# Second input projection by rows of the contraction, values by token, and one table slot for every side step

## The reference, cut to what matters

```python
h = rmsnorm_2(x, norm_mix_g[l])
proj = jnp.einsum('bsd,de->bse', h, w_in[l])          # 256 x 2048 by 2048 x 7568
c_q, c_kv, k_rope, dq, dk, dv, iq, ik, iw, gates = jnp.split(proj, splits, axis=-1)
# widths: 512, 256, 64, 1024, 256, 256, 1024, 64, 16, 4096
o_a = mla_branch(c_q, c_kv, k_rope, positions, ...)   # rmsnorm of c_q, c_kv; w_uq, w_uk, w_uv; rope; 8 heads
o_b = dsa_branch(dq, dk, dv, iq, ik, iw, positions)   # rope; index scores of 16 heads, top 64 keys of each query; 8 heads
merged = gate[:, :, 0, :] * (o_a @ w_branch_a[l]) + gate[:, :, 1, :] * (o_b @ w_branch_b[l])
x = x + merged @ w_out[l]                             # then the expert layer (peer_ffn) and a last rmsnorm
```

## Time and profile before

| | us |
|---|---|
| three runs | 3461.45, 3453.24, 3455.11 |
| median | 3455.11 |
| profiled execution, its own time | 3456.49 |
| its span in the trace | 3453.8 |
| mean granted TensorE clock | 0.991 |

### The profile page before, as it was taken

How to read it: one execution, slowest core, us unless ns; L and a number is a source line. 1 busy time by engine, 2 the same in 40 slices (tenths; PEclk the granted TensorE clock), 3 DMA queues, 4 the chain that set the end, 5 groups by cost and what they waited for, 6 DMA issues and landing times.

```text
span 3453.8 us, 60399 instructions
## 1 busy us (share of the span) xinstructions
PE 3401.8 (98%) x24920; PEld 3211.1 (93%) x24920; DVE 2205.4 (64%) x3713; ACT 1664.0 (48%) x2598; POOL 108.6 (3%) x141
## 2 busy tenths in 40 slices
PE   8999999999999989999999999999999999999998
PEld 8999999999999978999999999999999998887887
DVE  8775376666644477755566688878755555555655
ACT  5554454444434444444454444566644444444544
POOL 0000100000001010000000000022100000000000
PEclk9999999999999999999999999999999999999999
DMA  6433445555556644444565555544455555566554
GB/s 207 137 119 120 158 154 188 185 183 185 182 172 184 186 130 147 156 157 138 170 189 193 190 184 187 178 144 146 153 184 188 186 187 188 187 189 222 188 189 160
DMA packets 164000, 594.83 MB, mean 172 GB/s; under 512 B 18448, under 2 KB 19216, under 8 KB 163344
## 3 DMA queue, kind: packets, MB, share of 16 engines
q1 hardware_dynamic: 163728, 590.98, 52.4%
HBM read 586.71 MB, written 4.19 MB: 171 GB/s over the span
## 4 chain that ended last, share of the span: by engine, by line
PE 96%; DVE 2%; DMA 1%; ACT 1%; issue 0%; SPq 0%; ACTq 0%; DVEq 0%
PE ps L680 30%; PE ps L682 30%; PE ps L681 30%; PE ps L1130 2%; DVE wl L1202 1%; PE ps L747 1%; PE ps L954 0%; DMA raw<-in_peer_v 0%; PE ps L935 0%; PE ps L789 0%; PE ps L976 0%; ACT wh L1929 0%; PE ps L717 0%; DVE ht L1239 0%; PE ps L749 0%
## 5 line engine op out<-in xcount | busy, mean ns | idle before, releaser
L1929 ACT CAST wh<-raw 128x1024 fp32r<-128x1024 f32 (+1 forms) x1116 | 1161.0, 1041 | 1242.2 <-PE ps L682 1238.5
L1202 DVE TENSOR_TENSOR wl<-raw,wh 128x1024 fp32r<-128x1024 f32 (+1 forms) x1116 | 1351.8, 1212 | 523.9 <-ACT wh L1929 520.7
L680 PE MATMUL ps<-xh,wh 128*128 128x256 f32 (+2 forms) x5248 | 1511.1, 288 | 28.2 <-DVE wl L1202 14.9
L682 PE MATMUL ps<-xh,wl 128*128 128x256 f32 (+2 forms) x5248 | 1492.4, 284 | 0.0
L681 PE MATMUL ps<-xl,wh 128*128 128x256 f32 (+2 forms) x5248 | 1490.7, 284 | 0.0
L680 PEld LDWEIGHTS ps<-xh,wh 128*128 128x128 f32 x5248 | 1001.8, 191 | 39.4 <-issue 14.0
L681 PEld LDWEIGHTS ps<-xl,wh 128*128 128x128 f32 x5248 | 1000.2, 191 | 2.5
L682 PEld LDWEIGHTS ps<-xh,wl 128*128 128x128 f32 x5248 | 1001.7, 191 | 0.0
L680 PE MATMUL ps<-wh,ch 128*128 128x512 f32 x1024 | 406.6, 397 | 0.7 <-DVE cl L1866 0.7
L681 PE MATMUL ps<-wl,ch 128*128 128x512 f32 x1024 | 404.2, 395 | 0.0
L682 PE MATMUL ps<-wh,cl 128*128 128x512 f32 x1024 | 402.6, 393 | 0.0
(11 more groups left out here) (344 smaller groups left out, 3149.4 us busy)
## 6 DMA issues: line engine op xcount, KB each, us to landing
raw<-in_peer_u SPq DMA_DIRECT2D x256, 512.0 KB, 3.9
raw<-in_peer_v SPq DMA_DIRECT2D x256, 512.0 KB, 4.5
raw<-in_w_in SPq DMA_DIRECT2D x208, 512.0 KB, 3.8
raw<-in_w_up SPq DMA_DIRECT2D x82, 512.0 KB, 4.3
raw<-in_w_gate SPq DMA_DIRECT2D x80, 512.0 KB, 4.3
raw<-in_w_down SPq DMA_DIRECT2D x80, 512.0 KB, 3.8
raw<-in_w_out SPq DMA_DIRECT2D x64, 512.0 KB, 3.8
raw<-in_w_branch_a SPq DMA_DIRECT2D x16, 512.0 KB, 3.6
```

Of the source, the lines that this page charges most:

```text
L680: t.matmul(o, lh, rh, start=start, stop=False)
L682: return t.matmul(o, ll, rh, start=False, stop=stop)
L1202: v.tensor_tensor(wl[:, i % SN, 0:cols(i)], raw[:, i % RN, 0:cols(i)], wh[:, i % SN, 0:cols(i)].bitcast(F32), ALU.subtract).then_inc(lo, 1)
L1929: s.copy(wh[:, i % SN, 0:cols(i)], raw[:, i % RN, 0:cols(i)]).then_inc(hi, 1)
```

## The change

It has five parts. (1) `in2k`: 16 chunks of 128 x 896 hold row k of `cq` (4), `ckv` (2) and one joint tile `ki` (the 64 columns of `kr` and the 64 of `ik`), worked by rows as in GU; `pair` and `RAMP` are no longer used for this stage. (2) `svw`: `sv` and `iw` are computed by token, with `xh`, `xl` as the stationary side and 272 weight columns as the moving side, into `ps[0]` and `ps[1]`; no transposes. The inverse root by token comes from two transposes (`rcol`). (3) `ki` is spread to `kpe` and `ikT` by four permutation matmuls (`dup`). The tables times `r2` (`cosr`, `sinr`) let rope read PSUM without `read_2`; ACT copies the tile for PE (`copy`). (4) The `table` steps and the two sines run in the down stage; `positions` and `freq` are loaded at chunk `GU + 40`, `perm` and `kmask` at `I2 + 5`. (5) Each side step of each engine is its own entry in the table; `select` is 16 steps of one round; attention units take 4 slots' distance, `oa` first; DVE runs the side steps ahead of `cut(slot + 2)`. The exception for the last pair in `_sidesg` is gone.

```diff
+ROWS2 = [("cq", i) for i in range(4)] + [("ckv", i) for i in range(2)] + [("ki", 0)]
+GA = list(range(16)) + list(range(24, 32)) + list(range(16, 24))
+TILES2 = [("sk", i) for i in range(2)] + [("sq", i) for i in range(8)] + [("iq", i) for i in range(8)]
+TILES2 += [("ga", i) for i in GA]
+SVW = [(0, 3), (3, 3), (6, 3), (9, 3), (12, 2), (14, 2)]
+WV = 272
...
+PLAN += [("in2k", k, 0) for k in range(KT)] + [("in2", 0, c) for c in range(2)] + [("svw", c, 0) for c in range(len(SVW))]
+PLAN += [("in2", m, c) for m in range(1, IQ0) for c in range(2)]
...
     for f in range(FT):
         b = max(b, 4 * f + 4 if f > 3 else 0)
-        if f == FT - 1:
-            b = 4 * f + 2
...
+    for n in range(ROWS):
+        put(KT + n // 2, "row", n, 0.4)
+    put(18, "rcol", 0)
+    put(19, "rcol", 1, 0.2)
+    put(20, "rtab", 0, 1.1)
+    put(20, "latsq", 0)
+    put(21, "latsq", 1)
+    put(22, "latadd", 0, 0.55)
+    put(24, "latmm", 0)
+    put(24, "latmm", 1)
+    put(24, "sv", 0)
+    put(25, "latms", 0, 0.4)
+    put(25, "latms", 1, 0.4)
+    put(26, "latinv", 0, 1.8)
+    put(28, "latinv", 1, 1.8)
...
+        b = end2(m) + 1
+        put(b, "copy", m)
+        put(b if m else 21, "rope", m)
+        put(b + 1 if m else 21, "cos", m, 0.4)
+        put(b + 1 if m else 22, "sin", m, 0.8)
...
+    for u in range(16):
+        b = base + 4 * u
+        put(b, "score", u)
+        put(b + 1, "max", u, 0.55)
+        put(b + 1, "exp", u)
+        put(b + 2, "inv", u, 0.25)
+        put(b + 2, "scale", u)
+        put(b + 2, "turn", u)
+        put(b + 3, "tcopy", u)
+        put(b + 3, "mix", u)
+        put(b + 4, "high", u)
+        put(b + 5, "low", u, 0.4)
...
+    for r in range(8):
+        for qt in range(2):
+            while cost[slot] > 2.1:
+                slot += 1
+            put(slot, "select", (qt, r), 0.75)
...
+TABLES = [DN + 4 + 4 * i for i in range(7)]
...
-            if i == I2 + 14:
-                y.wait_ge(rs, RMS.index("x3") + 1)
+            if i == GU + 40:
+                y.dma_start(posi, A["pos"]).then_inc(d_pos, 16)
+                y.dma_start(freq[:, 0:3], A["freq"]).then_inc(d_frq, 16)
+            if i == I2 + 5:
+                y.wait_ge(rs, RMS.index("post2") + 1)
+                y.dma_start(perm[:], A["perm"]).then_inc(d_prm, 16)
...
+        def by_rows(i0, outs, rhs, norm, rows, T):
+
+            for k in range(KT):
+                taken(i0 + k)
+                t.wait_ge(xlo, 16 * norm + k + 1)
+                for n in range(ROWS):
+                    c = slice(128 * n, 128 * n + 128)
+                    last = three(outs[n], wh[:, (i0 + k) % SN, c], wl[:, (i0 + k) % SN, c], *rhs[n % 2](k), k == 0, k == KT - 1)
+                last.then_inc(gemm, 1)
+                if k == KT - 2:
+                    t.wait_ge(ms_add, norm + 1)
+                    mean_squares(ps[7][:, 0:T], [rows[:, 0, 0:T], rows[:, 1, 0:T]])
...
+        def by_token_2(i):
...
+            taken(i)
+            for k in range(k0, k0 + n):
+                c = slice(WV * (k - k0), WV * (k - k0) + WV)
+                for qt in range(2):
+                    tk = slice(128 * qt, 128 * qt + 128)
+                    last = three(ps[qt][:, 0:WV], xh[:, k, tk], xl[:, k, tk], wh[:, i % SN, c], wl[:, i % SN, c], k == 0,
+                                 k == KT - 1)
+            last.then_inc(gemm, 1)
...
-        pair(I2, [ps[0][:, 0:S], ps[1][:, 0:S]], [x3, x3], 2)
+        by_rows(I2, [ps[n][:, 0:S] for n in range(ROWS)], [x3, x3], 2, mt2, S)
...
+        for slot in range(KT, len(SIDES2)):
+            for name, a in SIDES2[slot]:
+                side_2(name, a)
             if slot < NS2:
                 cut(I2 + slot + 2)
...
+                if DN + 6 * m + c in TABLES[3::3]:
+                    i = TABLES.index(DN + 6 * m + c) // 3
+                    dst = snt if i == 1 else cst
+                    s.wait_ge(tab_a, i)
+                    s.activation(dst[:], dst[:], ACT.Sin).then_inc(tab, 1)
```

More of the change, by code:

```diff
@@ L332 @@
[L332 to L341 removed]
+    at = [[] for _ in range(NS2 + 8)]
@@ new lines, in _sides2 @@
+    put(28, "latinv", 1, 1.8)
+    put(30, "kmaskb", 0, 0.2)
+    slot = 0
+    for m in range(GA0):
+        if m == 1:
+            for i in range(2):
+                put(22 + i, "dup", i)
+                put(23 + i, "dupcos", i, 1.2)
+        b = end2(m) + 1
+        put(b, "copy", m)
+        put(b if m else 21, "rope", m)
+        put(b + 1 if m else 21, "cos", m, 0.4)
+        put(b + 1 if m else 22, "sin", m, 0.8)
+        if m >= IQ0:
+            for h in (2 * (m - IQ0), 2 * (m - IQ0) + 1):
+                slot = max(slot + 1, b + 1)
+                put(slot, "index", h)
+                put(slot + 1, "relu", h)
+                put(slot + 2, "weigh", h, 0.65)
@@ new lines, in _sides2 @@
+    chosen = slot + 3
+    up0 = AT["uqr", 0, 0] - I2
+    for n in range(4):
+        put(up0 + 2 + n, "rope", ("qr", n))
+        put(up0 + 3 + n, "cos", ("qr", n), 0.4)
+        put(up0 + 3 + n, "sin", ("qr", n), 0.8)
+    base = AT["uv", 1, 0] - I2 + 4
+    for u in range(16):
+        b = base + 4 * u
[9 more added lines that the diff above has]
+        put(b + 5, "low", u, 0.4)
@@ new lines, in _sides2 @@
+    for m in range(GA0, N2):
+        put(end2(m) + 1, "read", m, 0.4)
+    slot = 29
+    for q, n in ((0, 4), (1, 2)):
+        for i in range(n):
+            while cost[slot] + cost[slot + 1] > 4.6:
+                slot += 1
+            put(slot, "latn", (q, i), 0.45)
+            put(slot + 1, "latl", (q, i), 0.4)
+    slot = chosen
+    for r in range(8):
+        for qt in range(2):
+            while cost[slot] > 2.1:
+                slot += 1
+            put(slot, "select", (qt, r), 0.75)
@@ new lines, in _sides2, with order2 @@
+    return at, cost
+SIDES2, COST2 = _sides2()
+def order2(*names):
+    return [(n, a) for steps in SIDES2 for n, a in steps if n in names]
+READ2 = order2("row", "cos", "read")
+READ2 = [("in2" if n == "cos" else n, a) for n, a in READ2 if not (n == "cos" and isinstance(a, tuple))]
+READ2 = [("in2" if n == "read" else n, a) for n, a in READ2]
+COPIED = [m for _, m in order2("copy")]
+ROPED = [("dup", a) if n == "dupcos" else a for n, a in order2("sin", "dupcos")]
+assert ROPED == [("dup", a) if n == "dup" else a for n, a in order2("rope", "dup")]
@@ L342 @@
+SPREAD = [x for r in ROPED for x in ([(r, 0), (r, 1)] if isinstance(r, tuple) and r[0] == "dup" else [r])]
+WAITING = [0, "ki"] + list(range(1, IQ0)) + [("qr", n) for n in range(4)] + list(range(IQ0, GA0))
+TABLES = [DN + 4 + 4 * i for i in range(7)]
 UPS = []
@@ new lines, in dup_2, with rcol_2 @@
+        def dup_2(i):
+            t.wait_ge(ev2, READ2.index(("row", 6)) + 1)
+            free7((("dup", i), 0))
+            for part in range(2):
+                t.matmul(ps[7][:, 256 * part:256 * part + 256], perm[:, 3 + 2 * i + part, :], source2("ki"), start=True,
+                         stop=True).then_inc(rope_p, 1)
+        def rcol_2():
+            t.wait_ge(rs, RMS.index("x3") + 1)
+            t.wait_ge(ev2, READ2.index(("row", 3)) + 1)
+            for i in range(2):
+                last = t.transpose(ps[3][:, 128 * i:128 * i + 128], r2[:, 128 * i:128 * i + 128], ident[:])
+            last.then_inc(rcol_t, 1)
@@ L1579, in index_2, with row_2 @@
-        def index_2(h):
+        for i in range(DN, I2):
+            if i in TABLES:
+                tables(TABLES.index(i))
+            for name, f in SIDESG[i - GU] if i - GU < len(SIDESG) else ():
+                side_g(name, f)
+            cut(i + 2)
+        inverse_root("post2", ps[7][:, 0:S], D, EPS, tmp[:, 4, 0:S])
+        ramp(I2, 2, mt2, S, NM, "norm_mix_g_2", "x3", r2)
+        def row_2(n):
+            kind, h = ROWS2[n]
+            whole(I2 + KT - 1)
+            dst = source2("ki") if kind == "ki" else {"cq": cqs, "ckv": cks}[kind][:, h, :]
+            v.tensor_tensor(dst, ps[n][:, 0:S], r2, ALU.mult).then_inc(ev2, 1)
```

796 lines of the change are left out of this document (381 added, 415 removed).

## The result

| | before | after |
|---|---|---|
| median of four runs, us | 3456.95 | 3408.39 |
| lowest and highest | 3453.24, 3461.45 | 3407.02, 3409.22 |
| profiled execution, own time | 3456.49 | 3409.22 |
| its span | 3453.8 | 3407.4 |

The ratio is 0.9859, with a 95% interval from 0.9841 to 0.9876. In the spans that is 46.4 us less, where 37.2 were forecast; the median lies 0.6 us under the low end of the range.

A forecast was written before the change was run, and what follows sets the result against it. PE, busy 98% of the span, was taken as the bound. Terms of -10.8, +1.2, -10.2, -11.4 and -6.0 sum to -37.2 us, from a median of 3455.1 to 3418, with an 8-in-10 range of 3409 to 3434.

The forecast's parts named there:

- the five terms of the sum: Whole kernel: projections -10.8, small matmuls +1.2, ramp -10.2, after the ramp -11.4, end of GU -6.0; sum -37.2 us.
- the second of the first part: Any stretch's loss to waits and lower clock is its length less its matmuls times 0.1183 us.
- The stages at zero: Down, branches and output: forecast to change by zero; for down, at most 2 us if the cover failed.
- Projections and small matmuls: I2 on PE: fewer projection matmuls save 10.8 us; ropes, `dup`, latent means and transposes add 1.2.
- The ramp: I2's start: 21 matmuls a row instead of 6 cover DVE's row work; 3.0 us lost, so -10.2.
- After the ramp: I2 behind its ramp: waits from the order of ACT, DVE and DMA steps leave or spread; -11.4 us.
- The end of GU: Last pair: DVE's reading moves beside the down projection, ending stalls of 3.9 and 5.4 us; -6.0, at least 4.
- Tables in down: Down stage: seven table steps and the sines are covered by 3.4 us of lead; cost zero, at most 2.
- The order only moves the waits: Rival, I2: dense slots or selects fall behind, the 11.4 us after the ramp come back; 3429, chance 0.14.
- Lower clock: Rival, I2's ramp: cycling seven banks keeps PE at 1.2 GHz; 3447 us, chance 0.04.
- Slower, side steps ahead of the cut: Rival, slots 16 to 131: cuts wait for side steps, PE waits once a slot; 3476 us at 0.5, chance 0.04.
- The other signs: If right: ACT never over 3 us behind DVE in I2, no DVE wait at L1474 or L1485 before down.

The follow-up runs named there:

- e1: The kernel before with 32 unused bytes per partition behind `ht`, nothing else: 3441.55 us.
- e2: The kernel before with 6176 unused bytes per partition behind `ht`, exactly the address shift of the change without its work: 3443.49 us.
- e3: The kernel before with only the exception for the last pair in `_sidesg` taken out: 3446.82 us.
- e10: The changed kernel with rows 0 to 14 of I2's ramp multiplied for two tiles only, 225 matmuls left out (result incomplete): 3409.51 us.
- e7: The kernel before with tables and sines in the down stage and the mask copied at slot 30 of I2, buffers as in the change: 3432.57 us.
- e8: The changed kernel with the 16 `select` rounds in four lumps of four, four slots apart: 3406.78 us.
- e9: The changed kernel with DVE making `cut(slot + 2)` ahead of the slot's side steps, as in the kernel before: 3428.79 us.
- e17: e7 with DVE making the read-out and side steps of a slot ahead of `cut(slot + 2)` in I2: 3458.53 us.
- e13: e5 with 64 unused bytes ahead of `wh`, so weights and moving rows shift together: 3377.74 us.
- e6: The changed kernel with `xh`, `xl` rows 1024 bytes apart from I2 on, these and `ah`, `oa`, `mg` at 32 modulo 512: 3439.34 us.
- e5: The changed kernel with `xh`, `xl` rows 1024 instead of 1088 bytes apart from I2 on, at 480 modulo 512: 3377.70 us.
- e14: e5 with one to four small unused matmuls or transposes ahead of down's tiles, from the second on, none ahead of the last: 3373.94 us.
- e16: e5 with one unused transpose ahead of down's second tile and a fourth beside the three of each `pick` in U: 3364.53 us.
- e15: The kernel before with good places alone: the pad of e1 and the rows of e5: 3411.35 us.

## Why the prediction was wrong, point by point

The direction, the mechanism of the two rebuilt stages and each of the five terms of the sum were right to within two us, as far as the traces keep the terms apart. The total missed its range because of a price that I had held to be fixed.

**The step that failed** is the second of the first part: "With that price any stretch can be checked". I took 0.1183 from one full stretch of GU and used it for the whole kernel. It isn't a constant of the shape: the same 256 columns cost 0.1173 in the output projection of the same trace, which a look at one more window would have shown. From that followed the second failure, an edit that I costed at zero. The change allocates two tables ahead of `ah`, `oa`, `ob` and `mg`; I counted the instructions of that part and not its addresses. The stages at zero measured -2.0 (down), -3.1 (branches) and -3.1 (output), 8.1 of the 9.2 missing. The last two are the place: unused bytes alone give the same 3.1 and 3.1 (e1, e2). The 2.0 in down are not: taking the stall out at the old place gave 2.9 by itself (247.7, e3), and the changed kernel, at the new place, has 248.6. So by e3 what the zero for down left out is how the stage is entered, and the new place brought nothing there.

**The price itself was misread, and it was luck that this did little harm.** The 169 and 161 of the earlier trace rows count records that overlap the window. In that stretch of GU 167 matmuls start, 0.1198 apart, and nearly half of them have 258 columns; with 272 columns it is 159, 0.1261 apart. The 256-column matmuls of I2's tiles and of U happened to cost 0.1183, the number that the wrong count gave, so the terms of I2 came out.

**Projections and small matmuls**, -10.8 and +1.2: PE's records in I2 fell by 91; the forecast's count is 96 less, 8 more for the four float32 matmuls with two records each, 4 less for transposes, so 92 less. The token matmuls cost 0.126 where I had 0.1242, 0.1 us in all. A rope's matmul was put at 0.44, and 6.10 less 48 times 0.1183 is 0.42, which is nothing in the sum.

**The ramp**, -10.2: 315 matmuls in 38.72 us, 1.4 lost instead of 3.0, so -11.8. e10 shows the mechanism: with 6 matmuls a row it takes 35.1, so 15 more a row came nearly free. A row of DVE takes 2.19 with the cut that now comes with each; the 1.2 of the forecast held no cut, though the 35.5 us of DVE in GU's ramp, which it also names, did. It was still under the 2.5 of PE.

**After the ramp**, -11.4: what is left of I2's 33.9 when projections, small matmuls and ramp are taken off is 12.5, some 2 of it through the places (I2 is 2.1 shorter in e1, 2.6 in e2). So 10 to 11 by the order. Of its parts, tables and mask gave 6.2 (e7). The selects gave nothing that lumps of four don't give too (e8). The rest hangs on the new slot of every side step together with their order ahead of the cut; no run takes the two apart.

**The end of GU**, -6.0: -6.35 in the changed kernel, -6.9 alone (e3).

**Tables in down**: no cost in time, as forecast (239.3 in e7, 241.0 in e2 without them).

**The rivals.** "The order only moves the waits": no wait by a cut in I2 at all. "Lower clock": 0.96 over the ramp [0.93 in rows 4 for GU's]. The rule that the Trainium skill gives for cycling through banks (TensorE: Matmul & The Clock Gate, A second HAM failure mode: psum-queue depth-cycling) did not show with seven banks; the clock was down at 0.50 in e10, where two banks a row were used and PE stood between rows. "Slower, side steps ahead of the cut": the one that I misjudged in kind. I had the order as a risk of the new table; e9 shows that the new table loses 21 us without it, and e17 that the old table loses 23 with it.

**The other signs.** ACT's longest wait for DVE behind the ramp of I2 is 2.1 us, under the 3 named; no wait stands at the readings of the last pair.

**The range.** Without the 8.1 us of the three stages the time would be 3416.5, 1.5 under the forecast and inside its own range (the place alone brought 6.1 in branches and output and some 2 in I2, nearly the same sum). All ends of the range were made from the work that PE, DVE and ACT do; none held a change of price, whose spread over the stages (0.1173 to 0.1187 before, 1.2% of the 3,650 matmuls of down, branches and output) was in the trace.

## What to carry to other kernels

Take the price of a matmul from each stage before using it, at 100% busy and clock 1.00, and from the starts of its matmuls, not from the records that a window counts; where two stages of one shape differ, look at where the moving rows lie against the weights. Any new allocation ahead of a moving operand is an edit of the schedule of PE: bound it by the spread of prices that the trace shows, even if the instructions don't change. A side step that reads what the slot before has made goes ahead of the work that PE needs two slots later; one that waits for its own slot goes behind it.

## What the runs showed of the hardware

Not expected, with its numbers:

- An fp32r matmul of 256 columns with a new weight load each time costs 0.1133 to 0.1200 us at full clock, by the distance of the moving rows' address from the weights' (good at 192 modulo 256, the worst at 0, 96 and 128; a common shift of 64 bytes has no effect, e13). Over this kernel the worst place against the best is 3439 against 3378 us (e6, e5).
- The Trainium skill (SBUF — State Buffer, A bandwidth-pool intuition that's wrong) gives PE an independent second read port for weight loads. From that one would not expect the distance between the two addresses to matter, and here it does (3377.7 us in e5 and e13, 3439.3 in e6). That two reads of PE meet is the simplest reading of it; no run shows where. By the formula of the same skill's TensorE: Matmul & The Clock Gate, Back-to-back issue gap, the isolated gap is 109 ns for 256 columns. The best rhythm here is 4 ns above that, the worst place 11.
- At the good distance there are two stable rhythms, 0.1133 and 0.1178, kept over 2000 matmuls; one transpose can change between them (e14), though it did not in the traced execution of e16. At other distances there are two prices as well (0.1191 and 0.1167 at 496, 0.1187 and 0.1173 at 448).
- The stage behind a stall can get longer or shorter when the stall goes. At place 448 the stall's end took 6.9 us off GU and 2.9 off down (e3). At 480 GU was 5.8 shorter without it and down 9.3 longer (e15 to e5), two kernels that differ in more than the stall.
